# Decay exponents of a bidirectional scan: by half chunks, both directions stacked in one operand

## What is computed

```
Ad   = dt * A                                     # the steps, one per position and head
A_cs = cumsum(Ad) within a chunk
seg  = A_cs[l] - A_cs[s]                          # l >= s
Lmat = exp(where(l >= s, seg, -inf))
y_diag = (C @ B^T * Lmat) @ (x * dt)
states = B^T @ (x * dt * exp(A_cs[last] - A_cs))
y_off  = (C @ entering state) * exp(A_cs)
y    = y_forward + y_backward (the same on the flipped sequence, with its own dt and A) + x * d_skip
```

## Time and profile before

| | us |
|---|---|
| median of three runs | 2547.09 |
| lowest, highest | 2543.57, 2547.77 |
| profiled execution | 2544.5 |
| its span | 2541.8 |
| PE busy | 2438.0 |
| DVE busy | 1518.4 |
| ACT busy | 1316.0 |
| POOL busy | 631.5 |

### The profile page before, as it was taken

How to read it: one execution, slowest core, us unless ns; L and a number is a source line. 1 busy time by engine, 2 the same in 40 slices (tenths; PEclk the granted TensorE clock), 3 DMA queues, 4 the chain that set the end, 5 groups by cost and what they waited for, 6 DMA issues and landing times.

```text
span 2541.8 us, 34936 instructions
## 1 busy us (share of the span) xinstructions
PE 2438.0 (96%) x11436; PEld 1963.9 (77%) x11436; DVE 1518.4 (60%) x2563; ACT 1316.0 (52%) x1738; POOL 631.5 (25%) x733
## 2 busy tenths in 40 slices
PE   7999999999999999999899999999999999999997
PEld 6878787787877688887577787878877767888875
DVE  5789899998743311112659998989996442111126
ACT  5645555456464654344555455554645646444454
POOL 2424324143111011111124143432421111111110
PEclk9999999999999999999999999999999999999999
DMA  7567474755789588889564755746567876888893
GB/s 192 129 138 165 100 173 100 166 124 123 175 192 222 117 189 192 192 194 206 131 159 103 168 122 127 180 101 157 123 148 172 189 189 149 193 194 187 196 209 99
DMA packets 110700, 405.69 MB, mean 160 GB/s; under 512 B 12288, under 2 KB 12288, under 8 KB 110208
## 3 DMA queue, kind: packets, MB, share of 16 engines
q0 software_dynamic: 54144, 197.16, 46.0%
q1 hardware_dynamic: 55296, 202.66, 24.0%
q10 hardware_dynamic: 1152, 4.37, 0.5%
HBM read 402.04 MB, written 2.10 MB: 159 GB/s over the span
## 4 chain that ended last, share of the span: by engine, by line
PE 65%; DVE 17%; ACT 8%; issue 7%; DMA 2%; POOL 1%; ACTq 0%; DVEq 0%; SPq 0%; POOLq 0%
PE bank L749 19%; PE bank L751 19%; PE bank L750 19%; DVE tmp_m L1195 4%; DVE tmp_m L1191 2%; ACT w_lo L436 2%; DVE xs_b_c L1113 2%; ACT w_hi L435 1%; DMA w_raw<-w_stream 1%; PE bank L791 1%; PE bank L792 1%; PE bank L888 1%; PE bank L794 1%; DVE y_tok L1222 1%; DMA w_lo<-w_stream 1%
## 5 line engine op out<-in xcount | busy, mean ns | idle before, releaser
L328 POOL DMA_DIRECT2D w_lo<-w_stream x376 | 327.7, 878 | 1588.1 <-ACT w_lo L436 1523.9
L749 PE MATMUL bank<-x_hi,w_hi 128*128 128x512 f32 x1728 | 687.4, 398 | 8.4 <-DMA w_lo<-w_stream 8.4
L751 PE MATMUL bank<-x_hi,w_lo 128*128 128x512 f32 x1728 | 676.3, 391 | 0.0
L750 PE MATMUL bank<-x_lo,w_hi 128*128 128x512 f32 x1728 | 676.1, 391 | 0.0
L435 ACT ACTIVATE w_hi<-w_raw 128x1024 fp32r<-128x1024 f32 x378 | 398.1, 1053 | 299.8 <-PE bank L751 241.1
L436 ACT ACTIVATE w_lo<-w_raw 128x1024 fp32r<-128x1024 f32 x378 | 395.6, 1047 | 0.0
L749 PEld LDWEIGHTS bank<-x_hi,w_hi 128*128 128x128 f32 x1728 | 326.6, 189 | 80.9 <-issue 12.7
L750 PEld LDWEIGHTS bank<-x_lo,w_hi 128*128 128x128 f32 x1728 | 326.5, 189 | 71.1 <-issue 3.3
L751 PEld LDWEIGHTS bank<-x_hi,w_lo 128*128 128x128 f32 x1728 | 326.0, 189 | 69.4
L1113 DVE SCALAR_TENSOR_TENSOR z_a<-glu_out,conv_a_params,z_a 128x497 f32 (+14 forms) x480 | 320.1, 737 | 0.0
L1479 DVE TENSOR_TENSOR glu_out<-bank,sigmoids 128x512 f32<-128x512 f32 x44 | 30.4, 692 | 414.1 <-PE bank L751 414.1
(11 more groups left out here) (213 smaller groups left out, 3720.4 us busy)
## 6 DMA issues: line engine op xcount, KB each, us to landing
w_raw<-w_stream SPq DMA_DIRECT2D x378, 512.0 KB, 4.8
w_lo<-w_stream POOLq DMA_DIRECT2D x376, 512.0 KB, 7.4
z_b<-x_in SPq DMA_DIRECT2D x4, 512.0 KB, 6.3
w_ple_in<-w_ple ACTq DMA_DIRECT2D x2, 1024.0 KB, 11.1
out<-z_b SPq DMA_DIRECT2D x1, 2048.0 KB, 6.3
ple_p<-p_in ACTq DMA_DIRECT2D x2, 512.0 KB, 6.2
params<-par_in ACTq DMA_DIRECT2D x2, 340.0 KB, 3.1
tmp_m<-w_dt ACTq DMA_DIRECT2D x2, 256.0 KB, 5.2
```

The costliest lines, as they stand in the source:

```text
L328: gp.dma_start(wlo[:, s, :], w_stream[cyc, s].bitcast(F32R), accum_op=ALU.add).then_inc(lo_done[s], 16)
L749: pe.matmul(dst, wh, mh, start=first, stop=False)
L750: pe.matmul(dst, wh, ml, start=False, stop=False)
L751: return pe.matmul(dst, wl, mh, start=False, stop=last)
```

## The change

Within a chunk, let a half be 64 positions. For a target t in the early half, the forward exponents need only the forward steps of the early half, and so do the backward exponents need only the backward steps of the early half, plus, for a source in the late half, the sum of backward steps from position 64 up to the source, which doesn't depend on t. For the late half it is the mirror image.

- The two kinds of steps that a half needs, 64 rows each, are stacked in one operand of 128 rows. `masked_steps` writes 8 blocks of 64 columns (4 heads, two halves) for each part: one select over all 128 partitions, then one over the first 64, for high and low. Between the two pairs POOL waits for the first pair's end. `rhs_ready` counts twice a chunk.
- `exponent` has four matmuls of 256 columns: early half high and low, late half high and low, with the stationary `early_r` or `late_r`.
- `decay` is eight ACTIVATEs of 64 columns, 4 heads x 2 halves, each with a column of `gtab` (kind `EDGE`) as the bias.
- At the head of a layer `cumulative` has two more matmuls of 128 columns over 64 rows for the edge sums, and one of 256 columns with a permutation (`swap`) that exchanges the halves of the steps; `decays` has four more copies, and line 1344 waits for all six. DVE writes `swap` into a part of E.
- At the start POOL builds the two stationary triangles with four selects, and DVE's two casts go. The tables of steps are a sixth kind wide.

The diff, cut to its core (left out are declarations of semaphores and views, the new argument of `decay` where it is called, and `k=5` that becomes `KINDS`):

```diff
--- before.py
+++ after.py
@@ -82,11 +82,13 @@
 O_ALOG = O_DTB + 2 * HEADS
 O_DSK = O_ALOG + 2 * HEADS
 NPAR = O_DSK + HEADS
-DTK, ADT, WDEC, DOUT, TOT = range(5)
+DTK, ADT, WDEC, DOUT, TOT, EDGE = range(6)
+KINDS = 6
+HB = P // 2
 BWD, FWD = 0, 1
 LN_A, LN_1, LN_2 = range(3)
 NORMS = 3
-CONSTS = 15
+CONSTS = 19
 LOG_TERMS = 8
 E_BANKS = (6, 7, 4)
 
@@ -115,18 +117,17 @@
         zb = sb("z_b", [P, KT, T])
         sg = sb("sigmoids", [P, T])
         par = sb("params", [P, NPAR])
-        steps = sb("steps", [P, 5, 2, CH, HEADS])
-        gtab = sb("group_steps", [P, 2, 5 * 2 * CH, HG])
-        gad = sb("group_steps_split", [P, 2, 2, 2 * CH, HG], F32R)
+        steps = sb("steps", [P, KINDS, 2, CH, HEADS])
+        gtab = sb("group_steps", [P, 2, KINDS * 2 * CH, HG])
+        gad = sb("group_steps_split", [P, 2, 2, CH, 2 * HG], F32R)
         gpar = sb("group_params", [P, 2, GP])
         gdsk = sb("group_skip", [P, 2, HG])
-        nega = sb("neg_a", [P, 2 * HEADS])
         U = sb("tri_le", [P, P])
         LW = sb("tri_ge", [P, P])
         SL = sb("tri_gt", [P, P])
         SU = sb("tri_lt", [P, P])
-        SLR = sb("tri_gt_r", [P, P], F32R)
-        SUR = sb("tri_lt_r", [P, P], F32R)
+        early_r = sb("tri_early_half", [P, P], F32R)
+        late_r = sb("tri_late_half", [P, P], F32R)
         ones = sb("ones", [P, P])
         mean1 = sb("ones_over_d", [P, P])
         ident = sb("ident", [P, P])
...
@@ -332,12 +335,15 @@
 
                 gp.wait_ge(seg_done, seen(CH * G + c))
                 settle(gp)
-                for d, sign in ((FWD, 1), (BWD, -1)):
+                for rows, sign, base in ((P, -1, -HB), (HB, 1, 0)):
                     for part in range(2):
-                        ad = gad[:, q, part, d * CH + c, :].bitcast(F32).unsqueeze(2).broadcast_to([P, HG, P])
-                        i = gp.affine_select(out=rhs[:, d, part], in_=ad, compare_op=ALU.is_ge, fill=0.0, base=0,
-                                             pattern=[[0, HG], [sign, P]], channel_multiplier=-sign)
-                i.then_inc(rhs_ready, 1)
+                        ad = gad[0:rows, q, part, c, :].bitcast(F32).unsqueeze(2).broadcast_to([rows, 2 * HG, HB])
+                        i = gp.affine_select(out=rhs[0:rows, part], in_=ad, compare_op=ALU.is_ge, fill=0.0, base=base,
+                                             pattern=[[0, 2 * HG], [sign, HB]], channel_multiplier=-sign)
+                    i.then_inc(rhs_ready, 1)
+                    if rows == P:
+                        gp.wait_ge(rhs_ready, seen(2 * (CH * G + c) + 1))
+                        settle(gp)
 
             def skip(q, G):
 
@@ -381,6 +387,17 @@
             fill(SL[:, :], (0, 1, -1, ALU.is_gt))
             fill(SU[:, :], (0, -1, 1, ALU.is_gt))
             fill(ident[:, :], (0, 1, -1, ALU.is_equal))
+
+            def halves_of_sums(dst, early):
+
+                for rows, base, mult, step in ((P, HB if early else 0, -1, 1), (HB, 0 if early else HB, 1, -1)):
+                    gp.affine_select(out=dst[0:rows, :], in_=ones[0:rows, :], compare_op=ALU.is_gt, fill=0.0, base=base,
+                                     pattern=[[step, P]], channel_multiplier=mult).then_inc(consts, 1)
+                    n[0] += 1
+                    gp.wait_ge(consts, n[0])
+
+            halves_of_sums(early_r, True)
+            halves_of_sums(late_r, False)
             assert n[0] == CONSTS
             with gp.Fori(0, LAYERS) as L:
                 base = L * CYCLES
@@ -466,9 +483,15 @@
                 act.wait_ge(tr_done, seen(4 * G + 3))
                 act.activation(btok[:, :, :], quarters(bank[6]), ACT.Copy).then_inc(tok_evac, 1)
 
-            def decay(G, c):
+            def decay(q, G, c):
+                act.wait_ge(grp_ready, seen(G + 1))
                 act.wait_ge(seg_done, seen(CH * G + c + 1))
-                act.activation(E[:, c], quarters(bank[4 + c % 2]), ACT.Exp).then_inc(exp_done, 1)
+                for h in range(HG):
+                    for half in range(2):
+                        t, k = slice(half * HB, (half + 1) * HB), (2 * EDGE + half) * CH + c
+                        i = act.activation(E[:, c, h, t], quarters(bank[4 + c % 2])[:, h, t], ACT.Exp,
+                                           bias=gtab[:, q, k, h:h + 1])
+                i.then_inc(exp_done, 1)
 
             def state(G, n):
 
@@ -514,6 +537,12 @@
                 act.wait_ge(cum_done, seen(L + 1))
                 act.activation(stepf[:, WDEC:DOUT + 1, :], halves(bank[5]), ACT.Exp).then_inc(cum_exp, 1)
                 act.activation(stepf[:, TOT, :], bank[6][:, 0:GW], ACT.Exp).then_inc(cum_exp, 1)
+                swapped = bank[6][:, GW:].rearrange("p (d e) -> p d e", d=2)
+                for rows, to, of in ((slice(0, HB), BWD, FWD), (slice(HB, P), FWD, BWD)):
+                    act.activation(steps[rows, ADT, to].rearrange("p c h -> p (c h)"), swapped[rows, of, :],
+                                   ACT.Copy).then_inc(cum_exp, 1)
+                for half, b in ((0, bank[7]), (1, bank[4])):
+                    act.activation(stepf[:, EDGE, half * P:(half + 1) * P], b[:, 0:P], ACT.Copy).then_inc(cum_exp, 1)
 
             def pair(L, base, j, first=False):
 
...
@@ -822,18 +851,19 @@
 
             def exponent(G, c, first=False):
 
-                pe.wait_ge(rhs_ready, seen(CH * G + c + 1))
+                pe.wait_ge(rhs_ready, seen(2 * (CH * G + c + 1)))
                 if c == 0:
                     pe.wait_ge(yp_read, seen(CH * G))
                 elif c > 1:
                     pe.wait_ge(exp_done, seen(CH * G + c - 1))
                 if c == 1 or first:
                     pe.wait_ge(yl_done, seen(2 * G))
-                b = quarters(bank[4 + c % 2])
-                pe.matmul(b, SLR[:, :], rhs[:, FWD, 0], start=True, stop=False)
-                pe.matmul(b, SLR[:, :], rhs[:, FWD, 1], start=False, stop=False)
-                pe.matmul(b, SUR[:, :], rhs[:, BWD, 0], start=False, stop=False)
-                pe.matmul(b, SUR[:, :], rhs[:, BWD, 1], start=False, stop=True).then_inc(seg_done, 1)
+                for half, m in ((0, early_r), (1, late_r)):
+                    b = quarters(bank[4 + c % 2])[:, :, half * HB:(half + 1) * HB]
+                    f = slice((1 - half) * HG, (2 - half) * HG)
+                    pe.matmul(b, m[:, :], rhs[:, 0, f], start=True, stop=False)
+                    i = pe.matmul(b, m[:, :], rhs[:, 1, f], start=False, stop=True)
+                i.then_inc(seg_done, 1)
 
             def state(G, n):
 
@@ -909,7 +939,11 @@
                 a = stepf[:, ADT, :].rearrange("p (d e) -> p d e", d=2)
                 for o, d, m in ((0, BWD, SU), (1, FWD, SL), (2, BWD, LW), (3, FWD, U)):
                     pe.matmul(quarters(bank[5])[:, o, :], m[:, :], a[:, d, :], start=True, stop=True)
-                pe.matmul(bank[6][:, 0:GW], ones[:, :], stepf[:, ADT, :], start=True, stop=True).then_inc(cum_done, 1)
+                pe.matmul(bank[6][:, 0:GW], ones[:, :], stepf[:, ADT, :], start=True, stop=True)
+                pe.matmul(bank[7][:, 0:P], SU[HB:P, :], a[HB:P, BWD, :], start=True, stop=True)
+                pe.matmul(bank[4][:, 0:P], SL[0:HB, :], a[0:HB, FWD, :], start=True, stop=True)
+                pe.wait_ge(swap_ready, seen(L + 1))
+                pe.matmul(bank[6][:, GW:], swap[:, :], stepf[:, ADT, :], start=True, stop=True).then_inc(cum_done, 1)
 
             def pair(L, base, j, first=False):
 
...
@@ -1094,10 +1127,11 @@
                 step(dve.tensor_copy(gdsk[:, q, :], par[:, bass.ds(O_DSK + g * HG, HG)]))
                 step(dve.tensor_copy(gtab[:, q], src[:, :, bass.ds(g * HG, HG)]))
                 dve.wait_ge(dve_order, issued())
-                ad = gtab[:, q, ADT * 2 * CH:(ADT + 1) * 2 * CH, :]
-                step(dve.tensor_copy(gad[:, q, 0], ad))
+                ad = gtab[:, q, ADT * 2 * CH:(ADT + 1) * 2 * CH, :].rearrange("p (s c) h -> p s c h", s=2)
+                near, off = (gad[:, q, part].rearrange("p c (s h) -> p s c h", s=2) for part in range(2))
+                step(dve.tensor_copy(near, ad))
                 dve.wait_ge(dve_order, issued())
-                dve.tensor_tensor(gad[:, q, 1], ad, gad[:, q, 0].bitcast(F32), ALU.subtract).then_inc(grp_ready, 1)
+                dve.tensor_tensor(off, ad, near.bitcast(F32), ALU.subtract).then_inc(grp_ready, 1)
 
             def taps(outs, ins, ws, count, finish, between=lambda n: None):
 
...
@@ -1312,8 +1343,10 @@
                 dve.tensor_tensor(ty[:, 0, :].rearrange(dch, d=2, c=CH),
                                   bank[6][:, 0:GW].rearrange("p (c d h) -> p d c h", c=CH, d=2),
                                   bias.unsqueeze(2).broadcast_to([P, 2, CH, HEADS]), ALU.add).then_inc(dt_v, 1)
+                step(dve.tensor_copy(swap[:, 0:HB], ident[:, HB:P]))
+                dve.tensor_copy(swap[:, HB:P], ident[:, 0:HB]).then_inc(swap_ready, 1)
                 dve.wait_ge(nega_e, seen(L + 1))
```

(7 more changed lines are left out.)

39 lines of the change are left out of this document (19 added, 20 removed).

## The result

The changed kernel takes 2574.5 us (median of four, 2571.0 to 2577.5) where the kernel before takes 2547.4 beside it: ratio 1.0107, 95% interval 1.0092 to 1.0122. It is slower by 27 us, and outside the range of the prediction. The profiled execution took 2571.0 us.

What follows compares the result with a forecast made beforehand. The limit was taken to change hands between PE, DVE and ACT. Trips -2.4, clock -4.2, heads +1.8 and start +0.2 gave -4.6 from 2544.5: 2539.9, or 2543 on the median's scale; range 2535 to 2557.

Steps and rivals of the forecast that it cites:

- PE, exponent: TensorE's four exponent matmuls at 256 columns instead of 512: 1.02 us falls to about 0.57, 0.45 saved, 64 times.
- ACT, exponential: ScalarE's exponential as eight ACTIVATEs of 64 columns: 1.9 us a group where it was 0.60, +1.3, 64 times.
- The walk: One pair-loop trip followed in five steps: `L812` at +0.4 us, the trip's end at -0.3, eight trips -2.4.
- Rival B: ACT's longer groups are the path, `L812` 1.3 us late each trip: +8.2, 2555 us; chance 0.27.
- POOL: Four selects a chunk, two over 64 partitions, still 0.64 us each, plus a 0.1 to 0.2 wait between pairs.
- Rival C: POOL's own wait lets DVE leave `L1199` 1.3 us sooner: -1.2 a trip, 2535 us; chance 0.20.
- Step 2 of the walk: At `L1199` of chunk 1, POOL's selects start about 1 us earlier, so DVE enters at -0.9.
- Heads and start: More fp32 matmuls at each layer's head, +1.8 us in all; four more selects at the start, +0.2.
- The clock: Exponent (G1,3) behind the `L851` wait, at 1.2 GHz: another 0.85 us saved, five times, -4.2.
- PE's shorter work beyond that becomes waits: Beyond the -2.4 us in eight trips, TensorE's saving becomes waiting: `L878` from 0.71 to about 2.3 us.
- Rival D: No change: clock may fall in all eight trips, three more falls at `L851`, +5, so 2547 us; chance 0.08.
- all eight look alike, with a period of 151.34 us: The pair loop's eight trips, four a layer, were read as alike with a period of 151.34 us.

Runs made afterwards that it cites:

- b_pe256_fill: Kernel before with the exponent as four matmuls of 256 columns (each head's other direction left out) and idle matmuls in three TensorE waits: 2529.1 us, ratio 0.9928.
- b_pe256_fill_wait: As b_pe256_fill, plus GpSimd's wait in the middle of a chunk's four selects: 2526.4 us, ratio 0.9919 to the kernel before.

## Why the prediction was wrong

- **PE, exponent: right.** 0.55 us start to start (380.08 to 380.63) for a forecast of 0.57. With the clock held it is worth 9.5 us.
- **ACT, exponential: the size right, the place wrong.** A group takes 1.74 us, +1.15 for a forecast of +1.3. The walk set PE's lead of 0.9 against it and came to +0.4 at `L812`. With the clock held the short exponents are worth 0.3 us in A and the eight ACTIVATEs cost 1.1 (55.41 less 54.29). Rival B had this mechanism at 1.3 us a trip.
- **POOL: wrong.** I priced the select over 64 partitions by its own duration (two take 1.36 us, over 128 partitions 1.41) and its wait at 0.1 to 0.2 us (0.16). Both held. What the 64-partition form does to DVE where a skip product follows was not in the sum: some 8 us by the trips, 4 to 7 by ratios and times. The rows of before could not show it, as they have no such select. Rival C, that POOL's wait would let DVE in, had the right sign for the wait, but it is worth 0.3 us a trip (A -0.45, B +0.16), not 1.2.
- **Step 2 of the walk, DVE enters 0.9 earlier: failed.** `L1197` starts 29.18 us after the xs transposes (408.41 less 379.23), `L1163` did after 29.54 (250.48 less 220.94 in the same timeline of before): 0.36, and 0.49 in the mean of eight trips. The 3.37 us at `L1199` did go, but POOL's selects and the skip product of G0 come earlier. In three of eight trips, this one among them, the last instruction of DVE's convolution stands behind them, and its eight instructions take 9.53 us in place of 6.50; in the five others the convolution takes 7.32 and the weighted xs (`L1176`) stands 3.44. With selects over 128 partitions DVE enters 0.4 earlier without POOL's wait (`b_pe256_fill`, mean of the trips) and 1.1 earlier with it (`b_pe256_fill_wait`): PE's lead alone did not bring the forecast 0.9, and with the selects over 64 partitions in the kernel after 0.5 is left. The row of DVE's timeline before, and POOL's after:

```profile
232.50 6.50 DVE L1113 SCALAR_TENSOR_TENSOR xs_b_c<-conv_in,group_params,xs_b_c 128x510 f32<-128x510 f32 x8
```

```profile
396.06 1.50 POOL L341 TENSOR_SCALAR_AFFINE_SELECT seg_rhs<-group_steps_split 64x512 fp32r<-64x512 f32 x2 [0.16 <-POOL seg_rhs L341]
397.62 1.89 POOL L354 TENSOR_TENSOR y_tok<-x_tok,group_skip 128x1024 f32<-128x1024 f32 x1
```

- **Heads and start:** forecast +2.0; nothing that the traces can tell apart.
- **The clock: the step that failed most.** The sum had -4.2, because an exponent behind the wait at `L851` is cheaper at 1.2 GHz as well. Measured is +18: the loss to the clock goes from 9 to 27 us. The premise, "PE's shorter work beyond that becomes waits", was right, and I priced those waits at nothing. `L851`'s wait went from 3.13 to 4.4 or 4.5, with a low clock in all eight trips; `L869`'s went from 0.57 to 1.46 or 2.14 us and was followed by a low clock in six trips, `L878`'s from 0.71 to 2.13 or 2.25 and in four; at neither had the clock been low before. Rival D had it, and said that the clock may fall "at more places", but priced only "three more at `L851`, +5"; I gave it 0.08. The trips of before could have told the price of a fall: "all eight look alike, with a period of 151.34" was a misreading, since that is the period of a trip without a fall (C 19.56), and in the five trips with one C is 21.15 to 22.28. The warning of the Trainium skill that it cited ("TensorE: Matmul & The Clock Gate", section "HAM oscillation — how this bites in real kernels") is borne out here: idle matmuls in the waits brought back 27 us.

The sum as it should have been, per the runs: -9.5 (short exponent), +7.9 (exponentials), +10.5 (selects and the rest), +18 (clock) = +27. The terms are steps of one chain of kernels, so that they add up proves nothing, and by the intervals of the ratios each is uncertain by 3 to 6 us; the stretches of the trips give -8.9, +8.6, +8.1 and +18.2.

## What to carry to other kernels

Work taken from an engine that waits for others becomes waiting, and on TensorE longer waits can cost more than the work did: list every wait that grows, also those that show a full clock today, and price a fall at each. Before judging such a change, time both kernels with idle matmuls in the waits; here that turned a riddle of 27 us into 18 of clock and 9 of three other parts. An instruction on GpSimd is priced by what it does to VectorE beside it as well as by its own duration, and what follows it on GpSimd is part of that.
